# The S5 setup's TensorE step cut into six pieces that use the projection's PSUM banks

## The reference, cut to what matters

```python
def s5_mixer(u, h0_re, h0_im, lam_re, lam_im, b_re, b_im, c_re, c_im, d_skip, log_dt, w_glu):
    lam = lax.complex(lam_re.astype(f32), lam_im.astype(f32))
    dt = jnp.exp(log_dt.astype(f32))[:, None]
    a_bar = jnp.exp(lam * dt)
    b_bar = ((a_bar - 1.0) / lam)[:, :, None] * lax.complex(b_re.astype(f32), b_im.astype(f32))
    c_mat = lax.complex(c_re.astype(f32), c_im.astype(f32))
    ...
    _, h = lax.associative_scan(combine, (a_all, bu), axis=1)
    y = jnp.real(jnp.einsum('gcp,blgp->blgc', c_mat, h)).reshape(bsz, l_, BRANCH_W) + d_skip.astype(f32) * u
```

## Time and profile before

| | us |
|---|---|
| median of 3 runs | 1662.32 (1662.09 to 1666.46) |
| the profiled execution's own time | 1660.3 |
| its span | 1658.7 |
| TensorE busy, matmul / weight load | 1418.9 / 1243.1 |
| VectorE / ScalarE / GpSimd busy | 871.4 / 526.7 / 397.6 |

### The profile page before, as it was taken

The page is one execution under the profiler, slowest core; times in us unless marked ns, Lnnn a source line. Parts: engine busy times, 40 slices in busy tenths (PEclk is TensorE's granted clock), DMA queues, the critical chain, the costliest instruction groups (busy, mean ns, idle before and its releaser), DMA issues. The chain is left out here.

```text
span 1658.7 us, 31346 instructions
## 1 busy us (share of the span) xinstructions
PE 1418.9 (86%) x12439; PEld 1243.1 (75%) x12439; DVE 871.4 (53%) x2622; ACT 526.7 (32%) x1099; POOL 397.6 (24%) x404
## 2 busy tenths in 40 slices
PE   3666899979896898897999979997989899789877
PEld 2555698768685887886777869886878898779746
DVE  5975736363593626445736541636556534643444
ACT  4334423134323432212423343223532433321011
POOL 4221232432001342223210124243200333221001
PEclk7879898979897999886899989897999999879878
DMA  7122122322134334064322323243214414338101
GB/s 189 65 74 68 52 79 89 121 80 94 41 106 128 92 91 92 28 58 152 109 63 74 120 86 104 64 132 94 87 40 137 109 54 129 128 67 196 56 9 54
DMA packets 166792, 149.82 MB, mean 90 GB/s; under 512 B 63440, under 2 KB 155352, under 8 KB 164856
## 3 DMA queue, kind: packets, MB, share of 16 engines
q1 hardware_dynamic: 95928, 76.38, 16.9%
q10 hardware_dynamic: 70720, 71.44, 14.6%
HBM read 124.42 MB, written 23.37 MB: 89 GB/s over the span
## 5 line engine op out<-in xcount | busy, mean ns | idle before, releaser
L1033 POOL TENSOR_TENSOR wlo<-wraw,whi 128x512 fp32r<-128x512 f32 (+1 forms) x224 | 298.3, 1363 | 478.0 <-ACT whi L1080 477.9
L2214 PE MATMUL psum<-whi,hhi 128*128 128x256 f32 (+1 forms) x896 | 283.0, 316 | 37.3 <-DVE r L1497 16.4
L2214 PE MATMUL psum<-wlo,hhi 128*128 128x256 f32 (+1 forms) x896 | 272.5, 304 | 0.0
L2214 PE MATMUL psum<-whi,hlo 128*128 128x256 f32 (+1 forms) x896 | 272.3, 304 | 0.0
L2209 PE MATMUL psum<-hhi,whi 128*128 128x288 f32 (+2 forms) x672 | 230.0, 342 | 2.9 <-DVE hlo L1541 1.6
L2214 PEld LDWEIGHTS psum<-whi,hhi 128*128 128x128 f32 x896 | 191.8, 214 | 47.3 <-issue 44.3
L2209 PE MATMUL psum<-hhi,wlo 128*128 128x288 f32 (+2 forms) x672 | 218.9, 326 | 0.0
L2209 PE MATMUL psum<-hlo,whi 128*128 128x288 f32 (+2 forms) x672 | 218.7, 325 | 0.0
L2214 PEld LDWEIGHTS psum<-wlo,hhi 128*128 128x128 f32 x896 | 191.6, 214 | 0.7 <-issue 0.5
L2214 PEld LDWEIGHTS psum<-whi,hlo 128*128 128x128 f32 x896 | 190.7, 213 | 0.0
L2541 PE MATMUL psum<-wraw,mixT 128*128 128x256 f32 x768 | 177.2, 390 | 3.0 <-DVE xo L2139 3.0
(11 more groups left out here) (335 smaller groups left out, 2358.8 us busy)
## 6 DMA issues: line engine op xcount, KB each, us to landing
wraw<-in_w_in ACTq DMA_DIRECT2D x50, 1024.0 KB, 5.3
wraw<-in_w_out ACTq DMA_DIRECT2D x14, 1024.0 KB, 5.3
x<-xo SPq DMA_DIRECT2D x48, 128.0 KB, 2.3
r<-x SPq DMA_DIRECT2D x12, 512.0 KB, 4.3
r<-in_c_rot SPq DMA_DIRECT2D x4, 1088.0 KB, 7.0
wraw<-in_w_in ACTq DMA_DIRECT2D x4, 1056.0 KB, 5.7
r<-in_x_prompt SPq DMA_DIRECT2D x8, 512.0 KB, 4.8
r<-WTm SPq DMA_DIRECT2D x4, 1024.0 KB, 12.4
```

The source lines that it names most:

```text
L1033: nc.gpsimd.tensor_tensor(wlo[:, hslot[b], ks, 0:width], wraw[:, wslot[b], ks, 0:width], whi[:, hslot[b], ks, 0:width].bitcast(F32), ALU.s ...
L2214: mm = nc.tensor.matmul(bank.t[:, 0:width], x[:, kt, c], w[:, sl, kt, 0:width], start=first, stop=last)
```

## The change

Step w becomes six: t0 to t3 (four transposes each, one bank each) and k0 and k1 (32 small matmuls each, two banks each). They take their banks from the projection's three in rotation, not from `scores`, and each use frees its bank by its own copy. ScalarE copies 128x512 per t piece and 16x512 per bank of a k piece, as before. In pass 0 the t pieces stand between A0 and AX of the first HGRN2 chunk, and k0, k1 and s behind its A1. In pass 1, t0 and t1 follow output piece 13, t2 and t3 piece 14, and k0, k1 and s piece 15; the weave with the HGRN2 steps is then made over a list with more steps, so that its other members move too. WTm's store now waits for t3's copy, and Tm's for k1's two.

```diff
@@ make_plan
-    plan = first + spread(project(0, "hg", {"hg_f": [(("hgpre", 0), None)]}), s5set(0)[:-2]) + head[:k] + s5set(0)[-2:]
+    plan = first + spread(project(0, "hg", {"hg_f": [(("hgpre", 0), None)]}), s5set(0)[:8]) + head[:1] + s5set(0)[8:12] + head[1:k] + s5set(0)[12:]
...
-            filler = spread(outs(n), s5set(1)) if n == 0 else outs(n)
+            filler, rest = outs(n), s5set(1) if n == 0 else []
+            if rest:
+                filler = spread(filler[:13], rest[:8]) + filler[13:14] + rest[8:10] + filler[14:15] + rest[10:12] + filler[15:] + rest[12:]
...
+SET_PIECES = ("t0", "t1", "t2", "t3", "k0", "k1")
...
+            elif s[0] == "s5set" and part in SET_PIECES:
+                proj_uses += [s + (part, a) for a in range(1 + (part[0] == "k"))]
...
-            elif s[0] == "s5set" and part == "w":
-                score_keys += [s + (i,) for i in range(4)]
@@ SyncE
-                    sp.wait_ge(*scores.free.at(s + (1,)))
+                    sp.wait_ge(*PB[bank_of[s + ("t3", 0)]].free.at(s + ("t3", 0)))
                     sp.dma_start(WTm[l], cWT.rearrange("p q r x -> p (q r x)")).then_inc(*set_out.inc(s + (2,)))
-                    sp.wait_ge(*scores.free.at(s + (3,)))
+                    for a in range(2):
+                        sp.wait_ge(*PB[bank_of[s + ("k1", a)]].free.at(s + ("k1", a)))
@@ ScalarE
-                elif s[0] == "s5set" and part == "w":
...
+                elif s[0] == "s5set" and part in SET_PIECES:
+                    i = int(part[1])
+                    for a in range(1 + (part[0] == "k")):
+                        u = s + (part, a)
+                        bank = PB[bank_of[u]]
+                        act.wait_ge(*bank.full.at(u))
...
@@ TensorE
-                elif s[0] == "s5set" and part == "w":
+                elif s[0] == "s5set" and part in SET_PIECES:
+                    i = int(part[1])
+                    banks = [PB[bank_of[s + (part, a)]] for a in range(1 + (part[0] == "k"))]
                     pe.wait_ge(*set_dve.at(s + ("W",)))
-                    for ri in range(2):
-                        scores.claim(pe, s + (ri,))
-                        for q in range(8):
...
+                    for a, bank in enumerate(banks):
+                        bank.claim(pe, s + (part, a))
```

More of the change, by code:

```diff
@@ L206, in s5set @@
     def s5set(l):
-        return [(("s5set", l), x) for x in ("e", "e2", "e3", "b", "va", "vb", "wa", "wb", "w", "s")] if "s5" in parts else []
+        return [(("s5set", l), x) for x in ("e", "e2", "e3", "b", "va", "vb", "wa", "wb") + SET_PIECES + ("s",)] if "s5" in parts else []
     def s5(n, stages):
@@ L1247, in _ @@
                                 *(aux.free.inc(s + ("C",)) if ri == a == 1 else act_done.inc()))
-                elif s[0] == "s5set" and part == "w":
-                    for ri in range(2):
[L1250 to L1259, removed]
+                elif s[0] == "s5set" and part in SET_PIECES:
[4 more added lines that the diff above has]
+                        act.wait_ge(*bank.full.at(u))
+                        if part[0] == "t":
+                            nc.scalar.activation(cWT[:, i % 2 * 4:i % 2 * 4 + 4, i // 2, :], bank.t.rearrange("p (q x) -> p q x", q=4), ACT.Copy).then_inc(*bank.free.inc(u))
+                        else:
+                            nc.scalar.activation(cK[:, 8 * a + 4 * i:8 * a + 4 * i + 4, :], bank.t[0:16, :].rearrange("p (q x) -> p q x", q=4), ACT.Copy).then_inc(*bank.free.inc(u))
                 elif s in s5_x0.value and part == "w":
@@ L2224, in _ @@
                     mm.then_inc(*aux.full.inc(k))
-                elif s[0] == "s5set" and part == "w":
+                elif s[0] == "s5set" and part in SET_PIECES:
+                    i = int(part[1])
+                    banks = [PB[bank_of[s + (part, a)]] for a in range(1 + (part[0] == "k"))]
                     pe.wait_ge(*set_dve.at(s + ("W",)))
-                    for ri in range(2):
-                        scores.claim(pe, s + (ri,))
-                        for q in range(8):
[L2230 to L2233, removed]
+                    for a, bank in enumerate(banks):
+                        bank.claim(pe, s + (part, a))
+                    if part[0] == "t":
+                        for q in range(4):
+                            mm = nc.tensor.transpose(banks[0].t[:, q * P:(q + 1) * P], cW[:, i // 2, i % 2 * 4 + q].rearrange("p s c -> p (s c)"), ident)
+                        mm.then_inc(*banks[0].full.inc(s + (part, 0)))
+                    else:
                         for q in range(4):
                             for ri in range(2):
-                                for a in range(2):
+                                for a, bank in enumerate(banks):
                                     h = slice(64 * a, 64 * a + 64)
-                                    mm = nc.tensor.matmul(scores.t[0:16, a, q * P:(q + 1) * P], cBb[h, ri, 4 * r + q, :],
-                                                          cV[h, ri, 4 * r + q, 0:8].rearrange("p j c -> p (j c)"), start=ri == 0, stop=ri == 1)
-                        mm.then_inc(*scores.full.inc(s + (2 + r,)))
+                                    mm = nc.tensor.matmul(bank.t[0:16, q * P:(q + 1) * P], cBb[h, ri, 4 * i + q, :],
+                                                          cV[h, ri, 4 * i + q, 0:8].rearrange("p j c -> p (j c)"), start=ri == 0, stop=ri == 1)
+                                    if q == 3 and ri == 1:
+                                        mm.then_inc(*bank.full.inc(s + (part, a)))
                 elif s[0] == "s5" and part == "w":
```

## The result

| | us |
|---|---|
| before, median of 6 runs (1658.52 to 1666.46) | 1662.20 |
| changed, median of 6 runs (1638.97 to 1652.04) | 1644.44 |
| ratio, 95% interval | 0.9895 (0.9866 to 0.9924), 17.5 us faster |
| changed, measured again another time | ratio 0.9920 (0.9896 to 0.9944), 13.3 us faster |
| forecast | 1650.0, 12.5 us faster |

The account below looks back on a forecast made before the run. TensorE's work plus its waits was taken as the bound. Gains of 6.7 (pass 0) and 6.4 (pass 1) sum to 13.1, taken as 12.5: 1660.3 - 12.5 = 1647.8, plus 2.0 for the median, 1649.8, say 1650; range 1641 to 1657.

Parts of the forecast that it names:

- Pass 0, 6.7 us: Pass 0's setup: transpose copies cost nothing, k1 runs at half speed, chunk 0's scores start 6.7 us earlier.
- Pass 1, 6.4 us: Pass 1: 22.8 us of waits gone, 16.4 new, clock effects cancelled; gain 6.4 us, between 1 and 12.
- scores of chunk 2: Pass 1: new TensorE wait of 6.1 us, as A1 of chunk 2 is slowed by GpSimd's `wlo`.
- t3 for t1's copy: Pass 1: t3 needs t1's bank, whose copy stands behind AX and Q; new wait of 3.5 us.
- ml_ifg's third tile: Pass 1: the tile waits for the first take's bank, behind `whi` and the clearing; new wait of 4.4 us.
- the heap of stores: Pass 1: SyncE issues Em, VTm, WTm and Tm together from 526 on, costing ml_q's load 1 us.
- The collision of `wlo` with VectorE: Pass 1: GpSimd's `wlo` for ml_ifg overlaps A1 of chunk 2 and costs VectorE 4 us.
- k1's copies plus 8.3: Pass 1: Tm's stores end 8.3 us after k1's copies, as in pass 0, so clearing comes at 542.0.
- 1.8 + 1.5 for the setup's matmuls: Pass 1: transposes and small matmuls win about 1.8 + 1.5 us by full clock, cancelled against 3 to 4 lost.
- pass 1 gives nothing: Rival: pass 1's new waits weigh as much as the old, only pass 0's 6.7 remains; 1655.6 us, chance 0.22.
- Pass 1 keeps nearly all: Rival: `wlo` mostly avoids collisions and the load lands in time, pass 1 gives 12 or more; 1643, chance 0.17.
- The slower rival: Rival: pass 1's ml_q load lands 18 us late, holding ScalarE's takes of ml_ifg and TensorE; 1667, chance 0.04.

Follow-up runs that it names:

- thin_wlo: The full change, with GpSimd making the low parts of ml_ifg's weights in pass 1 for 8 columns instead of 264; 1640.18 us, ratio 0.9881 to the kernel before.
- late_load: The full change, with ml_q's weight load in pass 1 issued only when the T stores have landed, its split later too; 1639.86 us, ratio 0.9880 to before.
- t1_late_load: The full change, with pass 1's t1 right behind t0 and ml_q's load issued only after the T stores landed; 1640.22 us, ratio 0.9881 to before.
- early_stores: The full change, with pass 1's stores of E and VT issued right behind the V and W steps; 1643.67 us, ratio 0.9921 to the kernel before.
- early_load: The full change, with ml_q's weight load in pass 1 issued ahead of ScalarE's copy of k0; 1644.52 us, ratio 0.9917 to the kernel before.

## Why the prediction was right, and where it was not

*Pass 0, 6.7 us: right, step by step.* The copies of the transposes cost nothing, k1 starts behind k0's first copy at half speed (3.37 where I took 3.23), the scores no longer wait. 7.1 measured at the place and 7.8 (4.6 to 10.8) by the runs, so it is kept. The profile of pass 0's part alone agrees within the scatter of a single profile: its shift is 6.1 us behind the scores and 5.2 at the end.

*Pass 1, 6.4 us: the size was near (4.8 and 5.5), the working only in part.* I had 22.8 us of waits gone and 16.4 new. The gone ones are gone. The new ones are larger, term by term in the changed profile:

| term | forecast | measured |
|---|---|---|
| scores of chunk 2 | 6.1 | 4.25 |
| t3 for t1's copy | 3.5 | 6.87 |
| piece 14 for its bank | 0.8 | no wait |
| k for a copy | 0.6 | 0.76 |
| ml_ifg's third tile | 4.4 | 6.21 |
| the heap of stores | 1 | in the row above |
| left out: B0 of chunk 1 for VectorE, the sample tile, L2338 | 0 | 0.99, 1.28, 1.25 |

The collision of `wlo` with VectorE cost what I said, 4 us (3.9), but two steps later: I put it on A1 of chunk 2, and GpSimd, which is in order and had N of chunk 1 first (until 495.5), ran it beside A0 of chunk 3. So the wait ahead of t3 held the collision: without it (thin_wlo) it was 3.49, near my 3.5. And the wait ahead of chunk 2's scores, 6.1 by my sum, was 2.1 without the collision there; it measured 4.25, since t0 ended 0.7 us behind wb (488.40 against 487.68) where I had 2.7. The step that failed most is "k1's copies plus 8.3" for T's stores: they landed 13.0 us after the end of k1's copies at 522.4, which late_load puts down to ml_q's load, issued at 526.37 beside them: without it 9.4 us from the first issue, not 12.9. I had asked what the stores do to the load and not what the load does to the stores. And I took the third tile to wait for the take behind `whi`; it waited for the clearing.

The waits of pass 1 then net to 1.5 us, not 6.4. What made up for it is TensorE's clock. I had 1.8 + 1.5 for the setup's matmuls, which is the 3.3 measured, but cancelled it against 3 to 4 us lost behind the new waits, and there the other matmuls lost only 1.3 on average, inside their scatter. By the trace pass 1 is 1.5 + 3.3 - 1.3 = 3.5 us, by the runs 4.8 and 5.5. My waits were 5 us too good and my clock loss 2 us or more too high, so pass 0 was right by its mechanism, while the nearness of pass 1's size is in part luck. Rival "pass 1 gives nothing" fits the waits almost, and is excluded as a time by both runs of pass 1 alone. "Pass 1 keeps nearly all" gave 1643, which the first measurement, 1644.44, was nearer to than to my 1650; by its second measurement the change gives 13.3, and the sum of the parts 12.6 to 13.3, against my 12.5.

*The slower rival* (ml_q's load landing 18 us late) did not happen: the split behind the load started at 534.33, in good time for ml_q's first matmul at 549.10. Its direction was right in one thing, that this load and the setup's stores slow each other: T's stores took 9.4 us without it and 12.9 and 15.9 beside it.

## What to carry to other kernels

Count the waits over a stretch that holds the same matmuls in both programs, as length less busy time, and take the profile of an unchanged copy beside it. In the stretch used here they repeated within about 1 us, where its length differed by 7.5 us between two executions of one program by clock alone. Over the whole span they did not (239.8 and 234.0), so the stretch has to lie around the change. Then add up the changed step's own matmuls: a shorter wait ahead of them can show as their clock and not as a wait. When a step is cut in pieces over rotating buffers, look for the piece whose buffer is given back by an engine that first has a long step of its own, and move that piece ahead of it: here it was worth at least as much as pass 1's whole part. And where a load and a set of small stores overlap, ask which of the two someone is waiting for; the other can go later.

## What the runs showed of the hardware that I had not expected

One program's profiles differ by up to 7.5 us over 190 us, in busy time of TensorE (159.4 and 165.9 for the same 1582 matmuls) with the granted clock 0.91 and 0.87. A comparison of two edits can be hidden so: with both edits, 1.8 us less of waits and 3.0 us more of busy time. Why the clock differed there was not tried.

The eight T stores, 576 KB together, took 9.4 and 9.6 us with no weight load beside them (late_load, t1_late_load), 12.9 and 13.1 with a 1 MB load issued 4 us after the first of them (changed, early_stores), and 15.9 with that load issued 4 us ahead (early_load). WTm's store of 1 MB, ahead of them in the same queue, overlapped their start in changed, late_load and early_load, where it landed 8.4, 8.4 and 11.3 us after its issue.
